# Expert-choice encoder layer on one core: affinities written straight into the search table, a first gather with a signal of its own, and the final norm woven into the last expert

## The reference, cut to what matters

```python
h = rmsnorm(x, norm_mix);  x = x + token_mixer(h, ...)      # retention + dilated attention, gated
h = rmsnorm(x, norm_ffn)
aff = softmax(h @ w_router)                                  # 16 experts
gate, idx = top_k(aff.T, 64)                                 # each expert takes 64 tokens of each request
xs = h[idx]
hid = silu(xs @ w_gate) * (xs @ w_up)                        # 1024 -> 2048
out = (hid @ w_down) * gate                                  # 2048 -> 1024
x = x + scatter_add(out at idx)
y = rmsnorm(x, norm_final)
```

## Time and profile before

| | us |
|---|---|
| median of 3 runs (2620.83 to 2623.04) | 2620.89 |
| the profiled execution's own time | 2621.75 |
| its span, first to last instruction | 2619.3 |
| PE busy | 2487.9 |
| DVE busy | 1596.8 |
| ACT busy | 1375.3 |
| POOL busy | 386.7 |
| last expert's last matmul ends | 2586.7 |

### The profile page before, as it was taken

The page is one execution under the profiler, slowest core; times in us unless marked ns, Lnnn a source line. Parts: engine busy times, 40 slices in busy tenths (PEclk is TensorE's granted clock), DMA queues, the critical chain, the costliest instruction groups (busy, mean ns, idle before and its releaser), DMA issues.

```text
span 2619.3 us, 39067 instructions
## 1 busy us (share of the span) xinstructions
PE 2487.9 (95%) x13778; PEld 2148.7 (82%) x13778; DVE 1596.8 (61%) x1885; ACT 1375.3 (53%) x1512; POOL 386.7 (15%) x313
## 2 busy tenths in 40 slices
PE   7999999999979999999999399999999999999994
PEld 6998989788869998897788388888888888888883
DVE  3444444432334444444323588888888888888884
ACT  3434343432234343435332277777777777777774
POOL 2313122110113131221101200000000000000000
PEclk9999999999989999999999699999999999999997
DMA  4212121123232121211233699999999999999994
GB/s 165 88 37 86 48 88 49 57 81 144 97 131 80 57 88 48 88 48 58 81 117 114 237 376 384 385 386 382 389 385 391 384 377 393 380 381 394 385 373 172
DMA packets 129981, 550.22 MB, mean 210 GB/s; under 512 B 9088, under 2 KB 9216, under 8 KB 119664
## 3 DMA queue, kind: packets, MB, share of 16 engines
q1 hardware_dynamic: 122592, 522.81, 52.4%
q0 software_dynamic: 7312, 26.39, 3.4%
HBM read 528.20 MB, written 20.97 MB: 210 GB/s over the span
## 4 chain that ended last, share of the span: by engine, by line
PE 91%; DVE 3%; issue 2%; ACT 2%; DMA 1%; POOL 0%; SPq 0%; DVEq 0%; ACTq 0%; POOLq 0%
PE bank L946 40%; PE bank L705 30%; PE bank L721 10%; PE bank L736 4%; PE bank L820 2%; PE bank L975 2%; PE bank L757 1%; PE bank L788 1%; PE bank L768 1%; PE bank L809 1%; PE bank L910 1%; PE bank L793 1%; DVE w_lo L1402 1%; DMA w_raw<-in_w_b 0%; DVE y_tile L1849 0%
## 5 line engine op out<-in xcount | busy, mean ns | idle before, releaser
L1771 DVE TENSOR_TENSOR m_lo<-m_raw,m_hi 128x2048 fp32r<-128x2048 f32 x381 | 869.9, 2291 | 123.5 <-ACT m_hi L1307 121.6
L1307 ACT ACTIVATE m_hi<-m_raw 128x2048 fp32r<-128x2048 f32 x384 | 737.4, 1921 | 266.3 <-PE bank L946 266.3
L705 PE MATMUL bank<-w_hi,h_hi 128*128 128x256 f32 (+1 forms) x1536 | 490.3, 319 | 3.5 <-DVE h_lo L1578 1.8
L705 PE MATMUL bank<-w_hi,h_lo 128*128 128x256 f32 (+1 forms) x1536 | 475.1, 309 | 0.0
L705 PE MATMUL bank<-w_lo,h_hi 128*128 128x256 f32 (+1 forms) x1536 | 474.7, 309 | 0.0
L946 PE MATMUL bank<-m_hi,xs_hi 128*128 128x512 f32 x1040 | 324.1, 393 | 1.4 <-DVE xs_lo L1793 1.4
L946 PE MATMUL bank<-m_lo,xs_hi 128*128 128x512 f32 x1040 | 321.1, 390 | 0.0
L946 PE MATMUL bank<-m_hi,xs_lo 128*128 128x512 f32 x1040 | 321.1, 390 | 0.0
L705 PEld LDWEIGHTS bank<-w_hi,h_hi 128*128 128x128 f32 x1536 | 291.5, 190 | 32.1 <-issue 28.3
L705 PEld LDWEIGHTS bank<-w_lo,h_hi 128*128 128x128 f32 x1536 | 292.0, 190 | 0.0
L705 PEld LDWEIGHTS bank<-w_hi,h_lo 128*128 128x128 f32 x1536 | 291.5, 190 | 0.0
(11 more groups left out here) (188 smaller groups left out, 3466.0 us busy)
## 6 DMA issues: line engine op xcount, KB each, us to landing
m_raw<-in_w_exp_gate SPq DMA_DIRECT2D x128, 1024.0 KB, 7.9
m_raw<-in_w_exp_up SPq DMA_DIRECT2D x128, 1024.0 KB, 6.5
m_raw<-in_w_exp_down SPq DMA_DIRECT2D x128, 1024.0 KB, 7.4
w_raw<-in_w_b SPq DMA_DIRECT2D x24, 1536.0 KB, 6.4
w_raw<-in_w_a SPq DMA_DIRECT2D x24, 1024.0 KB, 4.8
w_raw<-in_w_c SPq DMA_DIRECT2D x24, 1024.0 KB, 4.8
w_raw<-in_w_d SPq DMA_DIRECT2D x8, 1024.0 KB, 4.9
xt<-in_x SPq DMA_DIRECT2D x8, 512.0 KB, 5.7
```

The source lines that it names most:

```text
L705: last = pe.matmul(ps_proj[:, proj.slot, 0:cols], a[:, c, tokens], v[:, c, :], start=c == n == 0, stop=c == chunks - 1 and n == 2)
L1307: act.activation(m_hi[slot.slot][:, :, :], m_raw[raw.slot][:, :, :], ACT.Copy)\
L1771: dve.tensor_tensor(m_lo[slot.slot][:, :, :], m_raw[raw.slot][:, :, :], m_hi[slot.slot][:, :, :].bitcast(F32), ALU.subtract)\
```

## The change

1. **Affinity table.** `aff_t` is gone. `aff_pad[0]` lies where it outlives the batches, is cleared once at the start, and the PSUM copy of each batch writes partitions 32 to 47 of it. At each batch's router stage, ahead of the normalised rows, DVE copies partitions 32 to 47 to 0 to 15, so that request 0's affinities move up before request 1's arrive.
2. **First gather.** Indexes are transposed ahead of values. DVE writes the first expert's column of indexes straight to `index_get` and signals `s_first`; POOL gathers on that, without its own copy. DVE's own early split now stands behind `xs_lo`.
3. **The end.** POOL gathers the last expert's rows of `y` (after the add of the expert before it) into `xs`. SP loads the eight tiles of `y` at the same point, into tiles with places of their own. ACT's squares and roots and DVE's inverses and multiplies for these tiles stand between the last four splits. The last expert's output times its gate plus `xs` is made by one DVE instruction into `hid`, normalised as one more tile, and scattered to the rows of `out` by an indirect DMA, once all eight tile stores have landed. In the last expert DVE makes two splits ahead of `hid` and two behind it.

```diff
+            then(dve.memset(aff_pad[0][:, :], 0.0))
             with rolled(dve, NB, t, PER_BATCH) as b:
...
+                then(dve.tensor_copy(aff_pad[0][0:NE, :], aff_pad[0][32:32 + NE, :]))
                 dve.wait_ge(s_gain, b * 32 + 32)
                 dve.wait_ge(s_rstd, b * 4 + 3)
                 normalised(0)
...
-                dve.tensor_copy(aff_t[:, bass.ds(b * T, T)].rearrange("n (q r) -> n r q", r=RES),
+                dve.tensor_copy(aff_pad[0][32:32 + NE, :].rearrange("n (q r) -> n r q", r=RES),
...
-            then(dve.memset(aff_pad[0][:, :], 0.0))
-            dve.tensor_copy(aff_pad[0][0:NE, :], aff_t[:, 0:T])
-            then(dve.tensor_copy(aff_pad[0][32:32 + NE, :], aff_t[:, T:2 * T]))
...
+            dve.tensor_copy(index_get[0:CAP, 0:1], index_t[:, 0:1])
+            dve.tensor_scalar(index_get[CAP:2 * CAP, 0:1], index_t[:, 32:33], float(T), None, ALU.add)\
+                .then_inc(s_first, 1)
...
+            transposed_lo(xs_hi, xs_lo)
             split_units(SPLIT_SLOTS - EARLY_SPLITS)
-            transposed_lo(xs_hi, xs_lo)
```

ACT, last expert, behind the split of C3:

```diff
+                transposed_hi(xs_hi)
+                act.wait_ge(s_scaled, START + NE - 1)
+                act.activation(gate_now[:, 0:1], m_gate[:, NE - 1:NE], ACT.Copy).then_inc(s_gnow, 1)
+                act.wait_ge(s_added_seen, START + NE - 1)
+                result_square(0)
+                result_square(1)
+                result_square(2)
+                result_roots(0)
+                split_units(1)
+                result_square(3)
+                split_units(1)
+                result_square(4)
+                result_roots(2)
+                split_units(1)
+                result_square(5)
+                split_units(1)
+                result_roots(4)
+                result_square(6)
+                result_square(7)
+                result_roots(6)
+                act.wait_ge(s_row, 1)
+                act.activation(scaled[:, :], hid[:, :], ACT.Square, accum_out=row_ms).then_inc(s_rowsq, 1)
+                act.wait_ge(s_rowvar, 1)
+                act.activation(row_ms, row_inv, ACT.Sqrt).then_inc(s_rowrstd, 1)
```

DVE, last expert:

```diff
+                split_units(2)
+                hidden_step()
+                split_units(2)
+                transposed_lo(xs_hi, xs_lo)
+                result_inverse(0)
+                result(0)
+                result(1)
+                split_units(1)
+                result_inverse(2)
+                split_units(1)
+                result(2)
+                result(3)
+                split_units(1)
+                result_inverse(4)
+                split_units(1)
+                result(4)
+                result(5)
+                result_inverse(6)
+                result(6)
+                dve.wait_ge(s_used, done.n())
+                dve.scalar_tensor_tensor(hid, ps_d, gate_now[:, 0:1], xs, ALU.mult, ALU.add).then_inc(s_row, 1)
+                result(7)
+                dve.wait_ge(s_rowsq, 1)
+                then(dve.tensor_scalar(row_inv, row_ms, 1.0 / D, EPS, ALU.mult, ALU.add))
+                dve.reciprocal(row_inv, row_inv).then_inc(s_rowvar, 1)
+                dve.wait_ge(s_rowrstd, 1)
+                dve.scalar_tensor_tensor(hid, hid, row_ms, final_gain, ALU.mult, ALU.mult).then_inc(s_rowout, 1)
```

SP and POOL, at the end:

```diff
-            sp.wait_ge(s_added, 16 * NE)
-            sp.wait_ge(s_mlo, UNITS)
+            sp.wait_ge(s_added, 16 * (NE - 1))
...
-            add(NE - 1, 2 * NE)
+            pool.indirect_dma_start(out=xs, in_=y, in_offset=...index_add...).then_inc(s_gather, 16)
+            for each in s_stored:
+                pool.wait_ge(each, 16 * NB * NT // 2)
+            pool.wait_ge(s_rowout, 1)
+            pool.indirect_dma_start(out=out rows, out_offset=...index_add..., in_=hid).then_inc(s_rows_stored, 16)
```

More of the change, by code:

```diff
@@ L198, in hybrid_encoder @@
         dist, _, _ = put("dist", [P, 2, 7 * P], F16)
+        tables_end = cursor[0]
         gain, _, _ = put("gain", [P, KC], F32)
@@ L202, in hybrid_encoder @@
         small, small_at, _ = put("small", [P, 64], F32)
-        aff_t, _, _ = put("aff_t", [NE, NB * T], F32)
+        aff_pad = [put(f"aff_pad{i}", [48, T], F32)[0] for i in range(2)]
         decay_cur = small[:, 0:2]
@@ L284, in hybrid_encoder @@
         final_gain, _, _ = put("final_gain", [P, D], F32)
+        y_tile = [put(f"y_tile{i}", [P, D], F32)[0] for i in range(2)]
         assert cursor[0] <= area
@@ L306, in hybrid_encoder @@
         scaled, _, _ = put("scaled", [P, D], F32)
+        y_tile += [put(f"y_tile{i}", [P, D], F32)[0] for i in range(3, 6)]
         assert cursor[0] <= area + 36864
+        cursor[0] = tables_at
+        y_tile += [put(f"y_tile{i}", [P, D], F32)[0] for i in range(6, NB * NT)]
+        assert cursor[0] <= tables_end
         bank = [ctx.enter_context(nc.psum_tensor(f"bank{i}", [P, 2, 512], F32)) for i in range(4)]
@@ L925, in _ @@
                 transposes([aff[:, i, :] for i in range(NT)], cols=NE)
-            for n, a in enumerate((best, best_f)):
+            for a in (best_f, best):
                 pe.wait_ge(s_best, 1)
@@ L1328, in after, with expert @@
                 done.k += units
-            def expert(e, last):
+            def expert(e):
                 after()
@@ L1339, in expert @@
                 split_units()
[L1340 to L1346, removed]
-                after()
-                if not last:
-                    split_units()
+                after()
+                split_units()
+                swish_step()
+                transposed_hi(hid_hi)
+                after()
+                split_units()
+                after()
+                split_units()
                 act.activation(gate_now[:, 0:1], m_gate[:, bass.ds(e, 1)], ACT.Copy).then_inc(s_gnow, 1)
@@ L1368, in _ @@
             with rolled(act, NE - 1, mt, per) as e:
[L1369 to L1382, removed]
+                expert(e)
+            last_expert()
         @block.vector
@@ L1798, in after, with expert @@
                 done.k += 4
-            def expert(last):
+            def expert():
                 after()
@@ L1812, in expert @@
                 split_units()
[L1813 to L1819, removed]
-                after()
-                if not last:
-                    split_units()
+                after()
+                split_units()
+                transposed_lo(hid_hi, hid_lo)
+                after()
+                split_units()
@@ new lines, in expert, with result_inverse, result @@
+                hidden_step()
+                after()
+                split_units()
+            def result_inverse(i):
+                two = slice(i, i + 2)
+                dve.wait_ge(s_ysq, i + 2)
+                then(dve.tensor_scalar(y_inv[:, two], y_ms[:, two], 1.0 / D, EPS, ALU.mult, ALU.add))
+                dve.reciprocal(y_inv[:, two], y_inv[:, two]).then_inc(s_yvar, 1)
+            def result(i):
+                dve.wait_ge(s_yrstd, i // 2 + 1)
+                dve.scalar_tensor_tensor(y_tile[i][:, :], y_tile[i][:, :], y_ms[:, i:i + 1],
+                                         final_gain[:, :], ALU.mult, ALU.mult).then_inc(s_yout, 1)
@@ L1836, in _ @@
             with rolled(dve, NE - 1, mt, per):
[L1837 to L1850, removed]
+                expert()
+            last_expert()
 def rope_tables():
```

105 lines of the change are left out of this document (81 added, 24 removed).

## The result

| | before | after |
|---|---|---|
| median, same chip (us) | 2621.97 (2620.83 to 2625.32, 4 runs) | 2596.15 (2594.89 to 2599.23, 4 runs) |
| profiled execution's own time | 2621.75 | 2597.14 |
| its span | 2619.34 | 2595.34 |
| last hidden step `hid` starts | 2559.56 | 2552.22 |
| last expert's last matmul ends | 2586.72 | 2579.79 |

The ratio is 0.9901 with a 95% interval of 0.9884 to 0.9918. The direction and the places were as forecast, the median lies 0.15 us above the range, and the forecast time of 2588.0 was missed by 8.

The account below looks back on a forecast made before the run. TensorE, busy 95% of the span, was taken as the bound, with gains only where it waits. 2621.75 less 12.05 (router end) and 20.8 (last expert) is 2588.9; less 0.86 to the median's scale, 2588.0 us; range 2584 to 2596.

Parts of the forecast that it names:

- Part 1, the search: Router end: without two table copies and the memset the search starts earlier, unslowed by POOL's splits; 8.5 us saved.
- The rival that the search waits for them: Router end: the search cannot start until POOL's splits end, at 1466.5; kernel takes 2601 us; chance 0.03.
- The added copies: Each batch, ahead of the normalised rows: a copy on the path costs 0.5 us, 1.0 in all (0.6 to 2.4).
- Part 2, the gather: First expert's gather: 2.85 us saved before it starts, 1.7 (0 to 1.7) in its landing on an empty queue.
- The start moves everything: Expert stage: the router end's 12.05 us reach the kernel's end, since the weight queue has room.
- the rival that weights bound it: Expert stage: weight loads are the bound, so the 12.05 us are lost and it takes 2600 us; chance 0.04.
- tile 0 has landed by about 2562: Last expert: after the gather, the first tile of `y` lands by about 2562, later tiles 1.3 us apart.
- If TensorE had no idle time at 2563 its clock should stay up: Last expert: TensorE no longer waits 1.20 us for `m_lo`, so its clock should stay at 1.00.
- The rival that TensorE starves among the D units: Last expert's last four units: late splits and a clock fall end TensorE 2.5 to 4 us later; 2590.5 to 2592; chance 0.15.
- DVE is the bound: Last expert: DVE's work, not TensorE's, sets the pace; TensorE ends 1.2 us earlier, at 2585.5.
- The end is at: Kernel's end: last store lands at 2592.9, then 0.8 and a 4.8 us scatter; ends at 2598.5, 20.8 us saved.

Follow-up runs that it names:

- e1: The changed kernel timed again with no edit: 2597.43 us, ratio 0.9904 to the kernel before.
- e4: The changed kernel with the added table copy moved off the path, behind the last router operand: 2591.75 us, ratio 0.9876 to the kernel before.
- e8: The changed kernel with DVE's early split put back ahead of `xs_lo`: 2602.28 us, ratio 0.9912 to the kernel before.
- e7: The changed kernel with POOL's gather from `y` held until tile 5 has landed: 2597.55 us, ratio 0.9900 to the kernel before.
- e2: The kernel before with only the new end, without the table and first-gather changes: 2610.70 us, ratio 0.9943 to the kernel before.
- e10b: The e9b kernel reordered: first of the last four splits ahead of the squares, the others as early as slots allow, results behind: 2591.32 us.
- e5: The changed kernel without POOL's own wait for the last scatter (SP still waits): 2593.39 us, ratio 0.9881 to the kernel before.
- e11b: The changed kernel with all of the last four splits ahead of the squares and results: 2600.00 us, ratio 0.9899 to the kernel before.
- e9b: The changed kernel with copy off the path, no POOL wait for the scatter, root table early, gather of `y` after tile 5: 2588.67 us.

## Why the prediction was right, and where it failed

**Part 1, the search: right.** "it starts some 0.2 us after the PSUM copy" and "I price this at nothing" hold: 0.1 us behind the copy's end, 8.62 saved for 8.5, and no round is longer beside POOL's splits. The rival that the search waits for them falls. The Trainium skill ("SBUF — State Buffer", Who interferes with whom) has a DVE instruction with at most one SBUF input, outside the modes that use both ports, stay clear of GpSimd; MAX8 reads `aff_pad` alone, and the trace agrees: 0.69 us beside POOL's splits and without them. FIND_INDEX8 and MATCH_REPLACE8 get `best` by an instruction of its own, read `aff_pad` alone too, and take no longer either.

**The added copies: the term that was mis-sized at the start.** "I take 0.4, and 0.1 for the wait behind it: 0.5 a batch, 1.0 in all (0.6 to 2.4)". The copy itself takes 0.43, as priced, and 0.66 with its handover. What was not in the sum is the engine that waits behind it: TensorE, whose idle time there grows from 1.90 to 2.56 and whose granted clock then stays at half longer. The two copies cost 2.65 by the profiles of e1 and e4 and 3.7 by the means over all profiles (5.7 by the medians of e1 and e4); in the profiled pair the router stages lost 1.96 and 1.63. A further 2.25 of the missing 4.8 is the slow first projection, which e1 shows to be no part of the change.

**Part 2, the gather: right in size, incomplete in its reason.** 2.69 from `best_f` to the gather (2.85 forecast) and 1.65 from the gather to the transposes (1.7). e8 shows that beside a DVE split the new gather would have paid 4.1, not 1.7. The first gather of before had no split beside it, so its 6.05 held none of this.

**"The start moves everything": right.** The expert stage lasts 1066.5 us with either start, so the rival that weights bound it falls.

**Part 3, up to the last matmul: the landing of tile 0 failed.** "tile 0 has landed by about 2562": on the clock of before it is 2564.4 (ACT's first square at 2557.05, with `hid` 7.34 earlier there). The tiles are issued from 2545.3, right behind the last weight loads, as forecast, and the queue moved 412 GB/s from 2544 to 2560, the forecast's rate; but they land 11.7 to 16.4 us after issue. The gather's share, 1.4 by e7, was in the forecast; what made the tile 2.4 late is open. The squares and the table load ahead of the first roots were in the forecast too. Result 0 starts at 2569.6 on that clock, 1.5 behind the forecast's 2568.1, and TensorE's end is 1.6 behind its 2585.5. "If TensorE had no idle time at 2563 its clock should stay up" held: the granted clock is 1.00 there. The rival that TensorE starves among the D units described the waits (1.56 and 1.24) and a TensorE end within 2 us of what came. In this profile the clock never fell, but in that of e2, with the same end, it did:

```profile
2580.65 0.69 PE L980 MATMUL bank<-m_hi,xs_hi 128*128 128x512 f32 x2 [2.71 <-DVE m_lo L1842]
```

Behind this wait the granted clock is 0.50 from 2582 to 2584, and TensorE ends 28.8 behind `hid`. Still the tail grew by only 1.2 us, 1.1 of it the later start of result 0. "DVE is the bound" is shown by this, by e10b and by the fixed 20.8 and 12.3 us above: the late tile cost the end what DVE did not catch up, 0.5 us at the last result (2590.4 on the clock of before, 2589.9 forecast), and TensorE's 1.6 cost it nothing.

**The end: a term was missing.** "Then 0.8 to the indirect DMA and its landing", and then "The end is at", with nothing between: the store landed in 2.61 (2.9 forecast) and the scatter in 3.4 (4.8), both better. But POOL waited for the landing and only then began a DRAIN of 4.73, 5.4 us from landing to the end in all. In the profile of before the DRAIN was to be seen, hidden behind the norm; moving the norm away laid it bare. This is the step that failed: the forecast priced POOL's ending at nothing, and it takes 5.4 us. On the path of DVE the miss behind `hid` is 0.5 for the last result, -0.4 for the store with its handover, -1.4 for the scatter and 5.4 for the DRAIN: 4.1 in all. e5 gives 2.5 back.

Together: 4.8 ahead of the experts (2.25 of it chance, most of the rest the two copies) and 4.1 behind the last `hid`, less 0.1, is the 8.85 that was missing. The scatter and the store were better than forecast, which hid 1.8 us of it: luck, as far as the number goes. Open is why TensorE's clock comes back at different times in runs of one kernel, which moves a profile by up to 3 us.

## What to carry to other kernels

When work that stood last is moved forward, list what ran hidden beside it, closing instructions of every engine too: one of them is last next. A short instruction on the path of TensorE costs more than its length where TensorE's clock is down or about to fall: here 0.66 us for each copy at full clock, and some 1.9 on average. When two engines interleave work at the end, count the idle time of the one that bounds; an earlier last matmul by itself brought nothing (e10b, e11b). Two edits that fill the same idle time do not add up (e9b). And before a single profile's difference is read, look where profiles of one kernel differ.

## What the runs showed of the hardware

- POOL's closing DRAIN behind an indirect DMA takes 4.6 to 4.8 us when the DMA has landed (before, after, e2, e11b) and 6.0 when it is being issued (e5, e9b, e10b). Waiting for the landing first only adds: 2.5 us.
- An indirect gather issued by POOL during DVE's subtraction of two SBUF operands of 128x2048 takes 3.00 us instead of 1.02 (e8) and 2.75 to 2.78 in 14 cases of the kernel before, until 0.8 to 0.9 us behind the subtraction's end; one that starts 0.13 us ahead of it takes 0.98. The Trainium skill ("SBUF — State Buffer", Who interferes with whom) infers that such an instruction of DVE leaves descriptor generation alone; this trace does not agree. Whether the wait is for writing descriptors or for reading the indexes is not shown.
- In two profiles of the same changed kernel the first projection's matmuls start 0.32 and 0.17 us apart, while the granted clock of the first one's window from 24 to 30 us is shown as 1.00. Seven of the fourteen profiles have the wider spacing. What slows them is open.
